# A two-layer hybrid trunk: the first loads in halves, ScalarE's rotary copies one level later, and the last scaling regrouped

## The chip, the cores and the metric

The kernel runs on one core of one Trainium2 chip. The metric is the device time of one execution in microseconds: the median of three runs was 838.24 us, from 836.58 to 839.73. All data is float32.

## What is computed

The reference is two layers and a last normalisation, on 256 tokens of 1024 features. Cut to what matters:

```python
def hybrid_layer(x, ...):
    h = rms_norm(x, norm_mix)
    proj = einsum('btd,dp->btp', h, w_in)       # 4120 columns
    y_gdn = gdn_mixer(...)      # 6 heads: conv, silu, l2norm, gated delta rule by chunks
    y_ret = retention_mixer(...)  # 4 heads: q and k are turned by rotary(), then retention
    y_mlstm = mlstm_mixer(...)  # 6 heads
    x = x + concat(y_gdn, y_ret, y_mlstm) @ w_out
    x = x + hierarchical_moe(rms_norm(x, norm_ffn), ...)   # 32 experts, top 2
    return x
# after both layers: rms_norm(x, norm_final)
```

`rotary(x)` returns `[x1*cos - x2*sin, x1*sin + x2*cos]` for the two halves x1, x2 of a head's 64 features. The gated delta rule needs the inverse of a unit lower triangular matrix for each head and half of the sequence.

## The kernel before, in words

The program is written engine by engine, with an explicit order in each engine's own queue and semaphores between them. An engine does what stands in its queue in that order; if one instruction waits, all behind it wait.

**Weights.** SyncE's queue (SP) issues nearly all loads. A slot holds 1 MB of weights (2048 float32 in each of 128 partitions). There are 12 ring slots and 12 more that are made from buffers free at the time. Each layer loads 24 slots of mixer weights (L484; `PROJ` gives their order: gdn 0, the small gates slot, gdn 1 to 4, gate 0 to 4, rqk 0 and 1, mv 0 and 1, mqk and so on) and 96 slots of expert weights (L511, three for each of 32 experts). A load waits until its slot was freed: `mix_freed` is counted up by TensorE, `moe_freed` by GpSimd. Among the loads SP also swaps the halves of the heads for the rotary step (`swap_halves`, L463 to L470: four small DMAs for the queries, before load 23 of the mixer, and four for the keys, before the third expert load); it waits there for ScalarE's copy (`rraw_ready`).

**The start.** SP loads the input as two halves of 512 KB (L461), then weight slot after weight slot, with the constants (1125 KB) after the third. ScalarE's queue loads `pars` (154 KB), the level masks (224 KB) and the router's weights (160 KB) at L1137 to L1139. ScalarE squares the two halves of x (L1146) while VectorE multiplies them with the gain into `hU` (L1434) and then sums the squares (L1443, L1444). TensorE's first product (gdn 0, L621) works on `hU`, which isn't normalised yet: the whole tile 0 (features k = 0 to 7), then k = 0 to 3 of tile 1, then the product with ones that gives the sum of squares (L629), then k = 4 to 7 of tile 1. ScalarE makes 1/rms from it (L1152, L1154), VectorE makes `hT` (L1448), and the products of all further slots (L597) read `hT`. A float32 matmul shows as two records of 256 columns in the profile, so 8 matmuls are "x16".

**The levels.** The inverse is built by doubling, in six levels (lev 1 to 6). In each, TensorE makes W (L800), transposes X (L780), runs half of a filler, makes Z (L813) and runs the other half of the filler. The filler is a product that the layer needs anyway: rqk 0 in levels 1 and 2, rqk 1 in levels 3 and 4, mv 0 in level 5, mv 1 in level 6. ScalarE copies the even columns of XT to XE before each level's transposes (L1234, two groups), waiting for VectorE's subtractions (L1625), and copies X out of PSUM behind the transposes (L1237). Behind L1237 ScalarE has one extra piece of work in each level:

```python
if lev == 2:
    rotary_in(0)                  # L1243: waits for rqk 0 in full, copies it (L1216)
if lev == 3:
    act.activation(mixT[:, 0:5, :], ..., ACT.Silu)
if lev == 4:
    rotary_in(1)                  # L1247
    act.preload_act_table_set(LN_EXP)
if lev > 4:
    values(("mv", lev - 5), ...)  # waits for the mv product of this level
```

VectorE turns the copies with cos and sin (`rotate`, L1587 to L1597) in level 4 for the queries and in level 6 for the keys, between its reads of W and its subtractions of Z; it waits there for the swapped halves (`partner_in`).

**The experts.** Both layers run eight groups of four experts, and one of them a second time for the tokens that did not fit, so 9 rounds in a layer. A round reads 12 slots, but the second turn of a group loads nothing.

**The end.** The last round leaves the result in PSUM banks 0 to 3 (bank 2j + h: token half j, feature half h). ScalarE squares them (L1377, L1380), makes 1/rms for j = 1 and then j = 0 (L1383, L1385). VectorE scales by 1/rms and gain in four operations (L1838), and SP issues one output DMA behind each (L516).

Of the kernel before, what the change touches and what calls it, by code (L numbers as in the profile page):

```python
# [30 lines left out]
P = 128  # L31
LAYERS = 2
D = 1024
# [12 lines left out]
RING = 12  # L46
SLOT = 2048
# [125 lines left out]
def trunk(nc, x_in, consts, level_masks, params, w_mix, router_w, e_gate, e_up, e_down, gain_final, row_store, out):  # L173
# [6 lines left out]
    with ExitStack() as ctx:  # L180
# [217 lines left out]
        const_in = sem("const_in")  # L398
        x_loaded = [sem(f"x_loaded{j}") for j in range(2)]
# [26 lines left out]
        out_ready = sem("out_ready")  # L426
        out_done = sem("out_done")
# [31 lines left out]
        def _(sync):  # L459
            for j in range(2):  # L460
                sync.dma_start(xT[:, 4 * j:4 * j + 4, :], x_in[:, 4 * j:4 * j + 4, :]).then_inc(x_loaded[j], 16)  # L461

# [9 lines left out]
            for l in range(LAYERS):  # L472
                for i in range(NMIX):
# [40 lines left out]
            for i, (j, h) in enumerate(((1, 0), (1, 1), (0, 0), (0, 1))):  # L514
# [39 lines left out]
        def _(pe):  # L554
# [52 lines left out]
            for l in range(LAYERS):  # L607
# [6 lines left out]
                have_slot(0)  # L614

                def first_tile(ct, ks):

                    for k in ks:
                        if ct == 0 and k % 2 == 0:
                            pe.wait_ge(hU_ready, upto(l, hU_ready, k // 2 + 1))  # L620
                        mm = pe.matmul(bank[:, ct * T:(ct + 1) * T], slot_w(0)[:, k, ct * P:(ct + 1) * P], hU[:, k, :],  # L621
                                       start=(k == 0), stop=(k == KD - 1))
                    return mm

                first_tile(0, range(KD))
                first_tile(1, range(4))
                sq_bank = begin("ssq")
# [472 lines left out]
        def _(act):  # L1100
# [37 lines left out]
            act.dma_start(lvl_raw, level_masks).then_inc(lvl_in, 16)  # L1138
            act.dma_start(rws[:, :, :], router_w[:, 0]).then_inc(rw_in, 16)  # L1139
            act.wait_ge(init_done, 2)  # L1140
            act.preload_act_table_set(LN_EXP)
            for l in range(LAYERS):
                if l == 0:
                    for i in range(2):
                        act.wait_ge(x_loaded[i], 16)
                        act.activation(sq_in[:, 4 * i:4 * i + 4, :], xT[:, 4 * i:4 * i + 4, :], ACT.Square).then_inc(squared, 2)  # L1146
                else:
# [79 lines left out]
                for lev in range(1, 7):  # L1227
# [14 lines left out]
                    if lev == 2:  # L1242
                        rotary_in(0)  # L1243
                    if lev == 3:
                        act.activation(mixT[:, 0:5, :], mixT[:, 0:5, :], ACT.Silu).then_inc(gate_ready, 1)
                    if lev == 4:
# [131 lines left out]
            for i, j in enumerate((1, 0)):  # L1378
# [6 lines left out]
                act.activation(ss[:, 4 + j:5 + j], ss[:, j:j + 1], ACT.Exp, scale=-0.5).then_inc(final_rstd, 1)  # L1385

        @block.vector
        def _(dve):
# [442 lines left out]
            dve.wait_ge(gfin_in, 16)  # L1831
            dve.wait_ge(final_sq, 2)
            dve.tensor_scalar(ss[:, 2:4], ss[:, 0:2], 1.0 / D, EPS, ALU.mult, ALU.add).then_inc(final_half, 1)
            for i, j in enumerate((1, 0)):
                dve.wait_ge(final_rstd, i + 1)
                for h in range(2):
                    part = slice(h * 512, (h + 1) * 512)
                    dve.scalar_tensor_tensor(out=fin[:, j, part], in0=ps[:, 2 * j + h, :], scalar=ss[:, 4 + j:5 + j],  # L1838
                                             in1=gfin[:, part], op0=ALU.mult, op1=ALU.mult).then_inc(out_ready, 1)
# [82 lines left out]
```

## Time and profile before

| what | us |
|---|---|
| median of three runs | 838.24 |
| the profiled execution | 839.36 |
| its span in the profile | 837.6 |
| PE busy (share of the span) | 783.1 (94%) |
| DVE busy | 307.2 (37%) |
| ACT busy | 201.3 (24%) |

PE is TensorE, DVE VectorE, ACT ScalarE, SP SyncE; PEq, SPq and so on are an engine's own queue. The durations below all come from the profiled execution, whose time stands 1.76 us over its span and 1.12 us over the median. The chain of waits follows the last instruction back to what released it, so its pieces add up to the span; the timeline lists what each engine did, with the idle time before it and what ended that in brackets; the waits sum idle time over an engine's instructions.

### The profile page before, as it was taken

To read this page: it belongs to the slowest core of one execution; us is meant where nothing else is said; L and a number is where in the kernel's file an instruction comes from. 1 tells how busy PE (TensorE), PEld (TensorE's weight loads), DVE (VectorE), ACT (ScalarE), POOL (GpSimd) and SP (SyncE) were. 2 spreads that over 40 slices of the span, in tenths; PEclk is the share of its full clock that TensorE was granted. 3 is DMA by queue.
4 is the path that set the end of the run, shared out by engine and by line. 5 is a ranking of instruction groups with operands and counts; after the bars stand their busy time and mean duration, and the time that the engine had idled before them with its cause. 6 is when DMAs were issued, how large, how long until landed. Compare 5 with 4: busy or idle time off the path is not lost.

```text
span 837.6 us, 16668 instructions
## 1 busy us (share of the span) xinstructions
PE 783.1 (94%) x6584; PEld 556.1 (66%) x6584; DVE 307.2 (37%) x733; ACT 201.3 (24%) x427; POOL 4.3 (1%) x13
## 2 busy tenths in 40 slices
PE   4999989999999998799999999899999999999966
PEld 4877778888765554455588778788787555454423
DVE  2757433564421111111177653436624111111102
ACT  2252551442300010001114445326212000001002
POOL 1000000000000000000000000000000000000000
PEclk9999999999999999699999999999999999999998
DMA  9851354486789999999996322645947999999995
GB/s 355 360 176 69 118 188 166 144 325 241 304 360 420 421 420 421 419 423 419 418 418 227 124 103 64 241 156 167 367 191 303 421 420 419 422 421 419 421 421 232
DMA packets 41065, 253.86 MB, mean 303 GB/s; under 512 B 4768, under 2 KB 9376, under 8 KB 11936
## 3 DMA queue, kind: packets, MB, share of 16 engines
q1 hardware_dynamic: 40416, 252.14, 75.4%
q8 instruction: 50, 0.82, 0.4%
q10 hardware_dynamic: 576, 0.72, 0.3%
q14 instruction: 23, 0.19, 0.1%
HBM read 250.35 MB, written 1.44 MB: 301 GB/s over the span
## 4 chain that ended last, share of the span: by engine, by line
PE 70%; DMA 11%; DVE 11%; ACT 3%; issue 3%; DVEq 1%; SPq 0%; ACTq 0%; POOLq 0%
PE ps L1049 13%; PE ps L597 12%; DMA ring<-e_up 10%; PE ps L1019 8%; PE ps L1070 7%; PE ps L921 6%; PE ps L768 4%; PE ps L1078 4%; PE ps L1082 3%; PE ps L813 2%; PE ps L621 2%; DVE xn L1421 2%; DVE work L1540 2%; PE ps L846 1%; PE ps L780 1%
## 5 line engine op out<-in xcount | busy, mean ns | idle before, releaser
L597 PE MATMUL ps<-hT,ring 128*128 128x256 f32 x800 | 183.4, 382 | 0.0
L597 PEld LDWEIGHTS ps<-hT,ring 128*128 128x128 f32 x800 | 148.3, 190 | 22.8 <-issue 3.8
L1019 PEld LDWEIGHTS ps<-work,xn 128*128 128x128 f32 x640 | 77.2, 201 | 10.3 <-issue 8.2
L1019 PE MATMUL ps<-work,xn 128*128 128x128 f32 x640 | 81.0, 288 | 1.9 <-DVE work L1759 1.9
L1049 PE MATMUL ps<-ring,hT 128*32 128x256 f32 x1088 | 67.0, 391 | 7.4 <-DMA ring<-e_up 7.4
L1049 PE MATMUL ps<-work,hT 128*32 128x256 f32 x960 | 59.9, 393 | 8.1 <-DMA work<-e_gate 5.7
L921 PE MATMUL ps<-xn,ring 128*128 128x256 f32 x256 | 57.8, 381 | 0.0
L1049 PEld LDWEIGHTS ps<-ring,hT 128*32 128x32 f32 x1088 | 34.5, 112 | 33.6 <-DMA ring<-e_up 10.5
L921 PEld LDWEIGHTS ps<-xn,ring 128*128 128x128 f32 x256 | 48.1, 190 | 7.2 <-issue 0.7
L1049 PEld LDWEIGHTS ps<-work,hT 128*32 128x32 f32 x960 | 28.9, 112 | 36.2 <-issue 12.1
L1759 DVE TENSOR_TENSOR work<-shapes,sel 128x128 f32<-128x128 f32 x40 | 9.9, 288 | 114.7 <-PE ps L1056 114.4
L1776 DVE TENSOR_TENSOR hT<-ps,pars 128x512 f32<-128x512 f32 x40 | 27.7, 692 | 52.9 <-PE ps L1019 52.9
L1364 ACT ACTIVATE work<-ps 128x256 f32<-128x256 f32 x18 | 6.9, 385 | 159.2 <-PE ps L1049 159.2
L1828 DVE COPY hT<-ps 128x512 f32<-128x512 f32 x18 | 12.4, 691 | 88.6 <-PE ps L1070 88.6
L1070 PE MATMUL ps<-ring,work 128*32 128x512 f32 x288 | 34.6, 598 | 8.5 <-ACT work L1368 8.5
L1368 ACT ACTIVATE work<-ps 128x256 f32<-128x256 f32 x18 | 6.9, 384 | 146.9 <-PE ps L1063 146.9
L768 PE MATMUL ps<-ring,hT 128*128 128x128 f32 (+1 forms) x256 | 37.5, 303 | 1.1 <-DVEq L1407 1.1
L1078 PEld LDWEIGHTS ps<-work,hT 128*128 128x128 f32 x144 | 25.1, 189 | 18.8 <-issue 7.5
L768 PEld LDWEIGHTS ps<-ring,hT 128*128 128x128 f32 x256 | 34.4, 191 | 3.9 <-DVEq L1407 1.9
L1078 PE MATMUL ps<-work,hT 128*128 128x256 f32 x144 | 36.1, 393 | 0.0
L1082 PE MATMUL ps<-hT,work 128*128 128x512 f32 x72 | 35.9, 621 | 0.0
L1625 DVE TENSOR_TENSOR work<-work,ps 128x192 f32<-128x192 f32 (+1 forms) x48 | 16.9, 353 | 33.7 <-PE ps L813 27.3
(283 smaller groups left out, 843.8 us busy)
## 6 DMA issues: line engine op xcount, KB each, us to landing
ring<-e_up SPq DMA_DIRECT2D x48, 1024.0 KB, 26.2
ring<-w_mix SPq DMA_DIRECT2D x34, 1024.0 KB, 9.6
ring<-e_down SPq DMA_DIRECT2D x32, 1024.0 KB, 26.0
work<-e_gate SPq DMA_DIRECT2D x32, 1024.0 KB, 20.2
more_buf<-e_gate SPq DMA_DIRECT2D x16, 1024.0 KB, 18.6
ring<-e_gate SPq DMA_DIRECT2D x16, 1024.0 KB, 18.7
work<-e_up SPq DMA_DIRECT2D x16, 1024.0 KB, 24.2
shapes<-e_down SPq DMA_DIRECT2D x8, 1024.0 KB, 21.9
```

What stands on the lines that cost most here:

```text
L597: mm = pe.matmul(bank, slot_w(i)[:, k, ct * P:(ct + 1) * P], hT3[:, k, :], start=(k == 0), stop=(k == KD - 1))
L621: mm = pe.matmul(bank[:, ct * T:(ct + 1) * T], slot_w(0)[:, k, ct * P:(ct + 1) * P], hU[:, k, :], start=(k == 0), stop=(k == KD - 1))
L768: mm = pe.matmul(bank[:, j * n:(j + 1) * n], hT3[:, k, j * P:(j + 1) * P], w[:, k, 0:n], start=(k == 0), stop=(k == KD - 1))
L813: mm = pe.matmul(z[j][0:rows_, i * HD:(i + 1) * HD], XC[half(j), h, 0:rows_], WC[half(j), h, :], start=True, stop=True)
L921: mm = pe.matmul(ps[:, b, i * T:(i + 1) * T], w[:, k, i * P:(i + 1) * P], mixT[:, k, :], start=(k == 0 and i == 0), stop=(k == KD - 1 and ...
L1019: mm = pe.matmul(ps[:, 4 + 3 * half_, kk * P:(kk + 1) * P], xn3[:, j, k * P:(k + 1) * P], Psel[:, j, :], start=(j == 0), stop=(j == TT - 1))
L1049: mm = pe.matmul(ps[32 * e:32 * e + 32, 5 + m, 0:DE], hq[:, k, 32 * e:32 * e + 32], w[:, c0:c0 + DE], start=(k == 0), stop=(k == KD - 1), ...
L1070: mm = pe.matmul(ps[32 * e:32 * e + 32, 5 + h, :], hmT[:, f, 32 * e:32 * e + 32], w[:, e * 512:(e + 1) * 512], start=(f == 0), stop=(f == ...
L1078: mm = pe.matmul(ps[:, k // 2, k % 2 * T:(k % 2 + 1) * T], ysb[:, h, k % 4 * P:(k % 4 + 1) * P], PwT[:, 0:T], start=False, stop=False, ski ...
L1082: mm = pe.matmul(ps[:, 2 * j + h, :], PwT[:, j * P:(j + 1) * P], ysb[:, h, :], start=False, stop=False, skip_group_check=True)
L1625: link(TTn(own, own, z, ALU.subtract))
L1776: TTn(hq[:, half * 4:half * 4 + 4, :], ps[:, 4 + 3 * half, :].rearrange("p (k s) -> p k s", k=4), gq[:, half * 4:half * 4 + 4].unsqueeze(2 ...
```

## The change

At the start the input and the first weight slot come in interleaved halves: x first half, weights first half, x second half, weights second half. TensorE first runs 10 products of the tile of ones with itself into bank 3, whose result is never read, then k = 0 to 3 of both tiles of gdn 0 from the first halves, and then k = 4 to 7 of tile 0; the rest follows as before. In layer 1 there is no split load and there are no such products, but the new order of k holds. The loads of the level masks and the router's weights move behind ScalarE's two squares.

In the levels the copy of the rotary queries moves from level 2 to level 3, ahead of the Silu, and the copy of the rotary keys from level 4 to level 5, together with the load of the activation table.

At the end VectorE multiplies the first feature halves (h = 0) with the gain before 1/rms is there, and scales the second halves with both as before. The first half of j = 1 is then scaled by 1/rms on VectorE, that of j = 0 on ScalarE, which also issues its output DMA; SP issues three.

```diff
             for j in range(2):
                 sync.dma_start(xT[:, 4 * j:4 * j + 4, :], x_in[:, 4 * j:4 * j + 4, :]).then_inc(x_loaded[j], 16)
-
+                part = slice(j * SLOT // 2, (j + 1) * SLOT // 2)
+                sync.dma_start(slot[first][:, part], w_mix[0, 0, :, part]).then_inc(arrived[first] if j else first_half, 16)
...
-                for i in range(NMIX):
+                for i in range(1 - l, NMIX):
...
-            for i, (j, h) in enumerate(((1, 0), (1, 1), (0, 0), (0, 1))):
+            for i, (j, h) in enumerate(((1, 1), (1, 0), (0, 1))):
...
-                have_slot(0)
+                if l == 0:
+                    for _ in range(WARM):
+                        pe.matmul(ps[:, 3, 0:P], ones[:, :], ones[:, :], start=True, stop=True)
+                    pe.wait_ge(first_half, 16)
+                else:
+                    have_slot(0)
...
-                first_tile(0, range(KD))
+                first_tile(0, range(4))
                 first_tile(1, range(4))
+                have_slot(0)
+                first_tile(0, range(4, KD))
...
             act.dma_start(pars[:, :, :], params).then_inc(par_in, 16)
-            act.dma_start(lvl_raw, level_masks).then_inc(lvl_in, 16)
-            act.dma_start(rws[:, :, :], router_w[:, 0]).then_inc(rw_in, 16)
...
                         act.activation(sq_in[:, 4 * i:4 * i + 4, :], xT[:, 4 * i:4 * i + 4, :], ACT.Square).then_inc(squared, 2)
+                    act.dma_start(lvl_raw, level_masks).then_inc(lvl_in, 16)
+                    act.dma_start(rws[:, :, :], router_w[:, 0]).then_inc(rw_in, 16)
...
-                    if lev == 2:
+                    if lev == 3:
                         rotary_in(0)
-                    if lev == 3:
                         act.activation(mixT[:, 0:5, :], mixT[:, 0:5, :], ACT.Silu).then_inc(gate_ready, 1)
-                    if lev == 4:
+                    if lev == 5:
                         rotary_in(1)
                         act.preload_act_table_set(LN_EXP)
...
+            act.wait_ge(final_rstd, 2)
+            act.wait_ge(gained_half, 2)
+            act.activation(fin[:, 0, 0:512], fin[:, 0, 0:512], ACT.Copy, scale=ss[:, 4:5]).then_inc(out_first, 1)
+            act.wait_ge(out_first, 1)
+            act.dma_start(out[:, 0, 0:512], fin[:, 0, 0:512]).then_inc(out_done, 16)
...
-            for i, j in enumerate((1, 0)):
-                dve.wait_ge(final_rstd, i + 1)
-                for h in range(2):
-                    part = slice(h * 512, (h + 1) * 512)
-                    dve.scalar_tensor_tensor(out=fin[:, j, part], in0=ps[:, 2 * j + h, :], scalar=ss[:, 4 + j:5 + j],
-                                             in1=gfin[:, part], op0=ALU.mult, op1=ALU.mult).then_inc(out_ready, 1)
+            dve.wait_ge(gfin_in, 16)
+            for j in (1, 0):
+                TTn(fin[:, j, 0:512], ps[:, 2 * j, :], gfin[:, 0:512], ALU.mult).then_inc(gained_half, 1)
+
+            def last_half(j):
+                dve.scalar_tensor_tensor(out=fin[:, j, 512:D], in0=ps[:, 2 * j + 1, :], scalar=ss[:, 4 + j:5 + j],
+                                         in1=gfin[:, 512:D], op0=ALU.mult, op1=ALU.mult).then_inc(out_ready, 1)
+
+            dve.wait_ge(final_rstd, 1)
+            last_half(1)
+            dve.wait_ge(gained_half, 1)
+            dve.tensor_scalar(fin[:, 1, 0:512], fin[:, 1, 0:512], ss[:, 5:6], None, ALU.mult).then_inc(out_ready, 1)
+            dve.wait_ge(final_rstd, 2)
+            last_half(0)
```

In the new code the wait for `gfin_in` stands behind the operation that halves the sums (`final_half`); before it stood ahead of it. The start flag of gdn 0 is set on its first product alone.

## Rows read from the trace of the kernel before

**Rows 1.** page of the profile: its head, and the DMA rate in 40 slices

```profile
span 837.6 us, 16668 instructions
...
GB/s 355 360 176 69 118 188 166 144 325 241 304 360 420 421 420 421 419 423 419 418 418 227 124 103 64 241 156 167 367 191 303 421 420 419 422 421 419 421 421 232
...
```

**Rows 2.** chain of waits, 0 to 60 us: start us, length us, what

```profile
...
1.65 8.79 DMA ring<-w_mix
...
10.53 7.54 PE ps L621 x24
18.07 0.43 PE ps L629 x2
18.50 1.73 PE ps L621 x8
...
```

**Rows 3.** timeline, 0 to 45 us: start us, length us, engine, line, names

```profile
...
0.87 0.10 POOL L523 MEMSET epsc<- 128x1 f32 x1
...
5.89 1.22 DVE L1434 TENSOR_TENSOR work<-xT,pars 128x1024 f32<-128x1024 f32 x1 [5.89 <-DMA pars<-params]
...
10.85 0.42 DVE L1444 TENSOR_TENSOR xn<-xn 128x256 f32<-128x256 f32 x1
...
```

**Rows 4.** instructions of L621 from 12.8 to 13.5 us: durations ns

```profile
...
L621 PE MATMUL ps<-work,ring x3: 631/631/631, 12.4 to 13.2; 128*128 128x256 f32 x3
...
```

**Rows 5.** instructions of L621 from 16 to 16.8 us: durations ns

```profile
...
L621 PE MATMUL ps<-work,ring x5: 379/379/379, 15.8 to 16.6; 128*128 128x256 f32 x5
...
```

**Rows 6.** the two input DMAs of L461: us from issue to landing

```profile
...
DMA to landing us min/median/max: 4.9/5.5/6.2
```

**Rows 7.** chain of waits, 84 to 137 us: levels' fillers, one stall

```profile
...
99.39 1.73 PE ps L597 x8
...
106.95 1.73 PE ps L597 x8
...
113.75 1.73 PE ps L597 x8
...
118.92 0.61 ACT work L1216
...
119.69 1.28 ACT L1248
...
122.59 1.79 PE ps L768 x16
...
```

**Rows 8.** waits of PE over the span: us in total, times, longest us

```profile
...
PE ps L780 <- ACT late_buf L1234: 6.9, 8, 1.9
...
```

**Rows 9.** timeline, 84 to 136 us, of ScalarE, SyncE and VectorE around the copies

```profile
...
105.23 2.69 SPq L470 DMA_DIRECT2D work<-late_buf  x4
...
109.21 1.27 ACT L1245 ACTIVATE xn<-xn 128x1280 f32<-128x1280 f32 x1
...
110.57 0.52 ACT L1234 ACTIVATE late_buf<-work 128x384 f32<-128x384 f32 x1
...
113.84 0.69 DVE L1591 TENSOR_TENSOR work<-work,shapes 128x512 f32<-128x512 f32 x1 [0.24 <-DVE work L1608]
...
119.59 2.57 SPq L470 DMA_DIRECT2D work<-work  x4
...
129.59 0.69 DVE L1591 TENSOR_TENSOR work<-work,shapes 128x512 f32<-128x512 f32 x1 [0.24 <-DVE work L1605]
...
```

**Rows 10.** DMA issues by line over the span: count, KB, median us to landing

```profile
...
work<-late_buf SPq DMA_DIRECT2D x8, 64.0 KB, 2.0
work<-work SPq DMA_DIRECT2D x8, 64.0 KB, 7.1
...
```

**Rows 11.** chain of waits, 812 to 838 us

```profile
...
790.40 26.73 DMA ring<-e_up
...
```

**Rows 12.** timeline, 815 to 838 us, the last results

```profile
...
832.30 2.73 DVE L1838 SCALAR_TENSOR_TENSOR work<-ps,ss,more_buf 128x512 f32<-128x512 f32 x4 [1.20 <-ACT ss L1385]
...
833.21 0.20 ACT L1385 ACTIVATE ss<-ss 128x1 f32<-128x1 f32 x1
```

More of the change, by code:

```diff
@@ L46 @@
 RING = 12
+WARM = 10
 SLOT = 2048
@@ L398, in trunk @@
         const_in = sem("const_in")
+        first_half = sem("first_half")
         x_loaded = [sem(f"x_loaded{j}") for j in range(2)]
@@ L426, in trunk @@
         out_ready = sem("out_ready")
+        out_first = sem("out_first")
+        gained_half = sem("gained_half")
         out_done = sem("out_done")
@@ L459, in _ @@
         def _(sync):
+            first = loads[0][0][0]
             for j in range(2):
                 sync.dma_start(xT[:, 4 * j:4 * j + 4, :], x_in[:, 4 * j:4 * j + 4, :]).then_inc(x_loaded[j], 16)
+                part = slice(j * SLOT // 2, (j + 1) * SLOT // 2)
+                sync.dma_start(slot[first][:, part], w_mix[0, 0, :, part]).then_inc(arrived[first] if j else first_half, 16)
             def swap_halves(a):
@@ L621, in first_tile @@
                         mm = pe.matmul(bank[:, ct * T:(ct + 1) * T], slot_w(0)[:, k, ct * P:(ct + 1) * P], hU[:, k, :],
-                                       start=(k == 0), stop=(k == KD - 1))
+                                       start=(k == 0 and ct == 0), stop=(k == KD - 1 and ct == 1), skip_group_check=True)
                     return mm
-                first_tile(0, range(KD))
+                first_tile(0, range(4))
                 first_tile(1, range(4))
+                have_slot(0)
+                first_tile(0, range(4, KD))
                 sq_bank = begin("ssq")
@@ L1829, in _ @@
                         dve.reg_add(rounds, rounds, 1)
-            dve.wait_ge(gfin_in, 16)
             dve.wait_ge(final_sq, 2)
             dve.tensor_scalar(ss[:, 2:4], ss[:, 0:2], 1.0 / D, EPS, ALU.mult, ALU.add).then_inc(final_half, 1)
-            for i, j in enumerate((1, 0)):
-                dve.wait_ge(final_rstd, i + 1)
-                for h in range(2):
-                    part = slice(h * 512, (h + 1) * 512)
-                    dve.scalar_tensor_tensor(out=fin[:, j, part], in0=ps[:, 2 * j + h, :], scalar=ss[:, 4 + j:5 + j],
-                                             in1=gfin[:, part], op0=ALU.mult, op1=ALU.mult).then_inc(out_ready, 1)
+            dve.wait_ge(gfin_in, 16)
[10 more added lines that the diff above has]
+            last_half(0)
 def kernel(**inputs):
```

## The prediction

> **What bounds the kernel now.** I read the page first. Its DMA line shows about 420 GB/s in most slices of the expert stages and much less in the mixers [rows 1], so what bounds has to be read stage by stage. The chain of waits comes next. In its first 60 us it is one DMA, weight slot 0, up to 10.4 us, and from 10.53 us TensorE's products with no gap [rows 2]. The chain of the levels is TensorE as well, but with a stretch of ScalarE inside: the copy of the rotary keys at 118.92 and a table load at 119.69, before TensorE's filler begins at 122.59 [rows 7]. Near the end of layer 1 the expert loads bound: the chain's step of 26.73 us is one of them, issued at 790.40 [rows 11]. The last 5 us are ScalarE's statistics and VectorE's four scalings [rows 12].
>
> Does time won early last? The saturated stretches begin when TensorE frees slots: before each of them the rate is lower (241 to 360 GB/s in slices 10 to 12, 191 and 303 in slices 30 and 31) [rows 1]. Their start moves with TensorE, and their length is given by bytes. So I take a shift of TensorE before them in full, in both layers. If I am wrong there, it is rival 3.
>
> **Part 1, the start.** Before, slot 0 was in at 10.44. The second x half was in at 1.19 + 6.2 = 7.4 and the first at 0.74 + 4.9 = 5.6 [rows 6]. VectorE's first hU took 1.22 us and was released by pars [rows 3]. Now the first x half and the first half of the weights stand where both x halves stood, 1 MB, and 384 KB of ScalarE's loads (masks, router) no longer run beside them. So the half weights are in by 7.4 at the latest. With x half 0 at 5.5 to 5.9 and 1.22 us for hU, TensorE can start between 6.7 and 7.4; I take 7.2.
>
> Prices of TensorE: 8 records take 1.73 us at the full rate [rows 2]. The first records lasted 631 ns against 379 ns later [rows 4, 5]: these are the two levels of the clock, 1.2 and 2.4 GHz, after an idle start. The first 24 records took 7.54 us against 3 x 1.73 = 5.19, so the slow start cost 2.35 us. The ten products of ones are 20 records of 128 columns, half of those above: 20 x 0.216 / 2 = 2.2 us at the full clock, 4.3 us at half. They can begin when GpSimd's two fills are done at 0.97 [rows 3], end near 5.4, and nothing waits for them; their cover is the wait for the first loads, and without it they would cost their 4.3 us. I take it that they bring the clock up and that it stays up over the idle 1.8 us to 7.2. No row shows such a gap at such a moment; the bounds are 0 and 2.35 us of loss.
>
> Then: 16 records from 7.2 to 10.7 (k = 0 to 3 of both tiles). The second x half now comes after 1.5 MB of SP's queue: slot 0 landed at 10.44 behind 2 MB, its last 512 KB take 1.25 us at 420 GB/s [rows 1] and the 384 KB of ScalarE's are gone (0.9), so 8.2; the whole of slot 0 near 9.5. The 8 records of tile 0, k = 4 to 7, run from 10.7 to 12.4 without a wait (hU for them: 8.2 + 1.22 = 9.4). The sum of squares was ready at 10.85 + 0.42 = 11.27 [rows 3], 3.9 us behind the second x half; so now at 12.1. The product with ones takes 0.43, the last 8 records 1.73: slot 1's work starts at 14.6, where it started at 18.50 + 1.73 = 20.23 [rows 2]. Gain 5.6 us. The sum of squares, near 12.1, caps it at 6.0; with the clock down it is 3.3. Slot gdn 1 is 2 MB + 128 KB + 1 MB into SP's queue, by 420 GB/s and slot 0's old landing about 12.9, ahead of 14.6. The constants (another 1125 KB) are wanted after two tiles and the gates, past 22. Masks and router weights, now issued near 9, are wanted tens of us later. In layer 1 the order of k changes nothing: the same 12 products stand ahead of the sum.
>
> A rule speaks against halving. By the Trainium skill, page "DMA: Bandwidth & Descriptors", section "Anatomy of one DMA — SWDGE (gpsimd) path", each DMA has a fixed part of about 2.0 us beside its bytes; if four DMAs paid it one after another, TensorE would start some 2 us later. The rows are against that here: the two x halves were issued 0.45 us apart and landed 1.8 us apart [rows 6], which 512 KB and ScalarE's share nearly fill by themselves.
>
> **Part 2, the rotary copies.** Level marks are the fillers' starts: 99.39, 106.95, 113.75, 122.59 [rows 7]. A level with no copy in its way is 113.75 - 106.95 = 6.80 us (level 3's filler to level 4's). Level 2 to 3 is 7.56, level 4 to 5 is 8.84. The excess is 0.76 and 2.04: the copy waits for the whole filler, then takes 0.61 (and the table load 1.28) ahead of the XE copies that the next transposes want. TensorE waited for XE copies 6.9 us in 8 places over the two layers [rows 8], so I take layer 1's levels to be like layer 0's. Moved one level on, a copy's source is long there and it runs in ScalarE's gap behind L1237. Gain 2.80 a layer, 5.6 us.
>
> What hides the moved work: in level 3 the Silu began at 109.21 and the XE copy at 110.57 [rows 9]; 0.65 us more ahead of it puts XE at 111.2, done 111.8, while the transposes come 0.8 us before the filler at 113.75, thus at 112.9. In level 5 copy and table load need 2.1 us before the mv copy, which waits 4 us for its product anyway.
>
> What comes late next is the swap of halves. SP issued the four queries' DMAs from 105.23 over 2.69 us, and each lands 2.0 after its issue [rows 9, 10]: 4.4 behind the copy. The copy now ends near 108.6 on the old marks, the swap at 113.0, and VectorE's rotate began at 113.84: 0.9 to spare. For the keys, copy end 122.2, four issues of 2.57 in all, landing near 126.5 to 127, also because three 1 MB loads stand ahead (7.1 from issue to landing before); rotate would begin at 129.59 - 2.04 = 127.6. Also hidden, by 0.6 or more. I cost both at nothing; without cover 0 to 1 us a layer, because VectorE would hold up its subtractions of Z. SP itself waits 3 us longer for the keys' copy with the expert loads 3 to 96 behind it. The third was not issued before 125.9, and the rate there was 144 to 188 GB/s (slices 6 to 8) [rows 1], so these loads catch up.
>
> **Part 3, the end.** VectorE's last operation ended at 832.30 + 2.73 = 835.03, with 0.68 each; the first 1/rms was there at 832.27, the second at 833.41 [rows 12]. Now two gain products (2 x 0.69) fill 831.1 to 832.5, then follow 0.68, the scaling in SBUF (no row; between 0.35 and 0.69, I take 0.5), and 0.68 with gaps of 0.05: 834.4. ScalarE scales its half from 833.4 to 834.1 and issues it meanwhile. The last DMA goes out 0.6 us earlier (0.3 to 0.8).
>
> **Sum.** 5.6 + 5.6 + 0.6 = 11.8 us, against the profiled execution 839.36 - 11.8 = 827.6. That one stood 1.12 over the median, so 826.4 for the median.
>
> **Rivals.**
> 1. The early products do not bring the clock up, or it falls again in the gap. For: the gap of 1.8 us, and the products' 4.3 us are hardly longer than the 4 us of slow records before [rows 2, 4]. Against: no row shows a fall after so short a gap. Price 2.35: 828.8. The Trainium skill ("TensorE: Matmul & The Clock Gate", "The HAM clock gate (the "warmup" mystery)") says that the slow start is a matter of time, not of the number of matmuls, and varies from run to run; by that, this rival would hold in some executions.
> 2. The swapped halves come late, and VectorE waits in levels 4 and 6. For: margins of 0.9 and 0.6 us. Price up to 1 us a layer: about 828.
> 3. The expert loads end the kernel on their own clock and take back what TensorE wins in front: the saturated stretches start no earlier. Then only part 3 and some of layer 0's stall remain, 837 or so. Against: the low rates ahead of them [rows 1].
> 4. Slower: SP stands at the wait for the keys' copy while slots are free, so expert loads are missing when a saturated stretch begins. Each 1 MB costs 2.5 us at 420 GB/s; five or more in all must be late to eat 11.8 us, and at seven the time is 843. It decides from the point where SP is held for 12 us or more beyond the free slots. I find 3 us against low rates.
>
> **How the numbers follow.** All three parts as worked: 0.55, time 826.4, alone 825 to 828. Rival 1: 0.2. Rival 2: 0.15. Rival 3: 0.07. Rival 4: 0.02. The last 0.01 is for a change that does nothing. The range takes in the first three with both together (831) and the bounds of the prices: 824.6 to 831.5. About 0.5% (4.2 us) is what a measurement of this kernel can tell from no change: faster 0.93, same 0.05, slower 0.02.
>
> **What would show it.** Right: the first L621 record near 7.2 at 379 ns, L597 starting near 14.6, all levels' marks 6.8 to 7 apart up to level 5, no ScalarE copy in the levels' chain, the fillers of layer 1 some 8.4 us earlier before its own levels, and saturated stretches of unchanged length. Wrong: L621 records of 631 ns after 7.2 (rival 1); an idle VectorE before L1591 with the swap as releaser (rival 2); the expert rounds' starts shifted but the end not (rival 3); lower DMA rates where they were 420 (rival 4).

## The result, and the profile after

| | before | after |
|---|---|---|
| median, us | 837.81 (4 runs, 836.58 to 839.73) | 827.47 (4 runs, 825.73 to 828.91) |
| profiled execution, us | 839.36 | 828.05 |
| its span, us | 837.6 | 826.2 |

The ratio is 0.9876, with a 95% interval from 0.9855 to 0.9897: between 8.6 and 12.1 us were won, where 11.8 us were forecast. Line numbers below are those of the changed kernel: L621 became L632, L597 became L603.

**The start.** The chain of waits of the changed kernel from 0 to 60 us (start, length, what) answers to [rows 2]:

```profile
...
6.93 7.02 PE ps L632 x24
13.94 0.43 PE ps L642 x2
14.37 1.73 PE ps L632 x8
16.10 3.71 PE ps L603 x16
...
```

TensorE's first real product starts at 6.93 instead of 10.53, but slot 1's work only at 16.10 instead of 20.23. That is 4.1 us, not 5.6. The timeline of the same stretch has the products of ones, and the two groups below it are the records of L632 from 9 to 10 and from 11 to 12 us, as [rows 4] and [rows 5]:

```profile
...
1.02 4.63 PE L622 MATMUL ps<-ones 128*128 128x128 f32 x20 [1.02 <-POOL epsc L529]
...
11.33 0.42 DVE L1462 TENSOR_TENSOR xn<-xn 128x256 f32<-128x256 f32 x1
...
```

```profile
...
L632 PE MATMUL ps<-work,ring x3: 634/634/634, 8.8 to 9.6; 128*128 128x256 f32 x3
...
```

```profile
...
L632 PE MATMUL ps<-work,ring x6: 379/379/379, 10.8 to 11.8; 128*128 128x256 f32 x6
...
```

Records of 634 ns still start at 9.6 us, 8.6 us after the products of ones began. The first 24 records took 7.02 us, where 5.19 is the price at the full clock: 1.8 us were lost in this execution, where it was 2.35 before. The lower clock is read from the records here. The profile's granted clock stands at 1.00 over the first 20 us of every kernel, also where the records are long.

**The levels.** The chain from 80 to 132 us, the levels' fillers as in [rows 7]:

```profile
...
95.27 1.73 PE ps L603 x8
...
102.06 1.73 PE ps L603 x8
...
108.85 1.73 PE ps L603 x8
...
115.64 1.79 PE ps L781 x16
...
123.11 1.79 PE ps L781 x16
...
127.72 3.46 PE ps L603 x16
...
```

The marks are 6.79, 6.79, 6.79 and 7.47 us apart; the levels 2 to 3 and 4 to 5 have lost their 0.77 and 2.05 us, and up to 115.64 no ScalarE stands in between. The last step, level 5 to 6, was 7.46 before too: the chain has ScalarE's copy of the mv product there, in both kernels. One thing came as not forecast. VectorE in level 6 (timeline, 76 to 132 us):

```profile
...
124.44 0.69 DVE L1609 TENSOR_TENSOR work<-work,shapes 128x512 f32<-128x512 f32 x1 [2.04 <-DMA work<-work]
...
```

It waits 2.04 us for the swapped keys, 1.4 us in layer 1. But the chain goes on from 127.72 at its old pace.

**The experts.** Some starts that can be laid over each other, us from the span's start:

| start of | before | after | earlier by |
|---|---|---|---|
| slot 1's first product | 20.22 | 16.09 | 4.1 |
| first product behind the levels, layer 0 (u1) | 137.96 | 131.01 | 6.95 |
| first expert product, layer 0 | 230.94 | 224.01 | 6.9 |
| layer 1's first product | 421.54 | 414.70 | 6.8 |
| u1, layer 1 | 546.85 | 537.20 | 9.65 |
| gather ahead of layer 1's experts | 636.08 | 626.43 | 9.65 |
| first expert product, layer 1 | 641.46 | 630.20 | 11.3 |
| last 16 records of L1049 (now L1062) | 817.18 | 805.90 | 11.3 |
| end of the last product | 831.85 | 820.47 | 11.4 |
| end of the span | 837.6 | 826.2 | 11.4 |

In this pair the shift of layer 0's start and levels goes through both layers unchanged, through both stalls on expert loads. But the table has a step that is no part of the change: 1.6 us between the gather and the first expert product of layer 1. The chain over the span, before and then after:

```profile
...
636.08 5.45 PE ps L1019 x32
641.53 3.59 PE ps L1049 x64
...
```

```profile
...
626.43 3.84 PE ps L1032 x32
630.27 3.59 PE ps L1062 x64
...
```

The same 32 records took 5.45 us before and 3.84 after: the execution profiled before ran them partly at the lower clock (granted 0.52 from 636 to 638 us and 0.63 from 638 to 640). It is a matter of the execution, as the experiments show. So the change as such was worth 9.8 us in this pair of profiles.

**The end.** The timeline of the last us, answering to [rows 12], and the landing of SP's three output DMAs and of ScalarE's:

```profile
...
820.92 0.75 DVE L1856 SCALAR_TENSOR_TENSOR work<-ps,ss,more_buf 128x512 f32<-128x512 f32 x1
...
822.06 0.72 ACT L1401 ACTIVATE work<-work,ss 128x512 f32<-128x512 f32 x1
822.06 0.75 DVE L1856 SCALAR_TENSOR_TENSOR work<-ps,ss,more_buf 128x512 f32<-128x512 f32 x1
822.81 0.38 ACTq L1403 DMA_DIRECT2D out<-work  x1
```

```profile
...
DMA to landing us min/median/max: 2.1/2.4/3.0
```

```profile
...
DMA to landing us min/median/max: 2.8/2.8/2.8
```

VectorE ends at 822.81, which is 2.34 us after TensorE's last product instead of 3.18. But the span's end is 5.73 us after that product, as against 5.75. The DMA rate in slices of 0.125 us, before from 833 us and after from 821.62 us, which is the same distance from the end of the last product (1.15 us):

```profile
...
GB/s 0 0 0 0 0 0 0 164 426 377 393 328 443 344 426 328 393 393 361 426 328 410 328 459 344 442 328 426 344 181 0 0 0 0 0 0 0 0 0 0
...
```

```profile
...
GB/s 0 0 0 0 0 0 0 164 442 344 393 377 426 328 360 393 360 426 361 426 344 410 377 393 360 426 328 394 361 197 0 0 0 0 0 0 0 0 0 0
...
```

The megabyte flows from the eighth slice to the thirtieth in both. With the four DMAs closer together each one only takes longer to land, up to 3.0 us instead of 2.1.

### The profile page after: what moved, and what is told of

Same layout as the page of the kernel before. It is cut to its first block, busy times and chain, and to the rows that moved or that the text cites. A ratio compares the mean times of both kernels' runs of the same rounds, so it can differ in the third digit from the quotient of the medians.

```text
span 826.2 us, 16713 instructions
## 1 busy us (share of the span) xinstructions
PE 784.9 (95%) x6604; PEld 557.0 (67%) x6604; DVE 307.7 (37%) x734; ACT 201.9 (24%) x428; POOL 3.1 (0%) x13
## 3 DMA queue, kind: packets, MB, share of 16 engines
HBM read 250.35 MB, written 1.44 MB: 305 GB/s over the span
## 4 chain that ended last, share of the span: by engine, by line
PE 68%; DMA 15%; DVE 11%; issue 3%; ACT 3%; DVEq 0%; SPq 0%; ACTq 0%; POOLq 0%
DMA ring<-e_up 14%; PE ps L603 12%; PE ps L1062 11%; PE ps L1032 7%; PE ps L1083 6%; PE ps L934 6%; PE ps L781 4%; PE ps L1091 3%; PE ps L1095 3%; PE ps L826 2%; PE ps L632 2%; DVE xn L1439 2%; DVE work L1558 2%; PE ps L859 1%; PE ps L793 1%
## 5 line engine op out<-in xcount | busy, mean ns | idle before, releaser
L603 PE MATMUL ps<-hT,ring 128*128 128x256 f32 x800 | 183.4, 382 | 0.0
L603 PEld LDWEIGHTS ps<-hT,ring 128*128 128x128 f32 x800 | 148.3, 190 | 22.9 <-issue 3.8
L1032 PEld LDWEIGHTS ps<-work,xn 128*128 128x128 f32 x640 | 74.4, 195 | 10.3 <-issue 8.2
L1032 PE MATMUL ps<-work,xn 128*128 128x128 f32 x640 | 78.2, 281 | 1.9 <-DVE work L1777 1.9
L1062 PE MATMUL ps<-ring,hT 128*32 128x256 f32 x1088 | 67.2, 391 | 4.9 <-DMA ring<-e_up 4.8
L1062 PE MATMUL ps<-work,hT 128*32 128x256 f32 x960 | 60.7, 397 | 10.4 <-DMA work<-e_gate 5.7
L1062 PEld LDWEIGHTS ps<-ring,hT 128*32 128x32 f32 x1088 | 34.4, 112 | 32.0 <-DMA ring<-e_up 9.0
L1062 PEld LDWEIGHTS ps<-work,hT 128*32 128x32 f32 x960 | 29.1, 113 | 38.9 <-issue 12.6
L1843 DVE TENSOR_TENSOR work<-work,ps 128x256 f32<-128x256 f32 x18 | 7.6, 421 | 57.7 <-PE ps L1062 57.7
```

Of the source, the lines that this page charges most:

```text
L603: mm = pe.matmul(bank, slot_w(i)[:, k, ct * P:(ct + 1) * P], hT3[:, k, :], start=(k == 0), stop=(k == KD - 1))
L1032: mm = pe.matmul(ps[:, 4 + 3 * half_, kk * P:(kk + 1) * P], xn3[:, j, k * P:(k + 1) * P], Psel[:, j, :], start=(j == 0), stop=(j == TT - 1))
L1062: mm = pe.matmul(ps[32 * e:32 * e + 32, 5 + m, 0:DE], hq[:, k, 32 * e:32 * e + 32], w[:, c0:c0 + DE], start=(k == 0), stop=(k == KD - 1), ...
```

## The experiments

Each kernel of this study also has GpSimd clamp its loaded count of extra rounds at zero:

```diff
+            nclamp = pool.alloc_register("pool_clamp")
...
-                    pool.reg_add(rounds, rounds, nreg)
+                    pool.reg_alu(nclamp, nreg, 0, ALU.max)
+                    pool.reg_add(rounds, rounds, nclamp)
```

The ratio of times is always to the kernel before on the same chip, with its 95% interval.

**The start alone.** The hunks of the change for SP's first loads, TensorE's first tile and ScalarE's loads, put into the kernel before.

> The kernel before with the change at the start alone. GpSimd clamps its loaded count at zero in every kernel of this study, which is one register operation in eight places of a layer and off TensorE's path. Theory A (a shift of TensorE ahead of the saturated loads is kept to the end): slot 1's work starts near 16.1 us instead of 20.2, and the time is 3.5 to 4.5 us under that of before. Rival B (the expert loads end the kernel on their own clock): the same start, but less than 1 us in the time. In both, the records of the first product last 631 ns for some 3 us after 6.9 us.

Measured: 833.35 us against 837.56, ratio 0.9959 (0.9941 to 0.9977), 3.4 us (1.9 to 4.9). Its timeline from 0 to 14 us:

```profile
...
6.87 5.42 PE L632 MATMUL ps<-work,ring 128*128 128x256 f32 x24 [1.21 <-DVE work L1447]
...
```

Here the 24 records took 5.42 us, close to the full clock, and slot 1's work started at 14.45. The expectation, taken from the one profile after, missed that; the prediction's 14.6 was right for this execution. Its u1 came 117.84 us behind slot 1's start (before 117.74), and from the first expert product of layer 1 to the last product of the up weights it took 175.7 us, like before: behind slot 1's start this profile kept the shift. The time is another matter. Slot 1's work started 5.8 us earlier than in the profile before, but the time fell by 3.4 us, and the interval ends at 4.9. The profiled execution was the fastest of the ten (831.31 us, the others 832.43 to 835.97), so it need not stand for them. The granted clock over the whole span, known for each execution, was 0.980 to 0.982 in the four slowest (835.30 us and more) and 0.984 to 0.989 in the six others: clock losses behind the start, which differ from execution to execution, are in these times too.

**The rotary copies alone.** The hunks in ScalarE's levels, put into the kernel before.

> The kernel before with the two rotary copies one level later, alone. Theory A: each layer's levels are 2.8 us shorter, 5.6 us in the time; VectorE waits 1 to 2 us for the swapped keys in level 6 of each layer, and it costs TensorE nothing because the first product behind the levels covers it. Rival B (late loads take it back): 2.8 us or less in the time. Rival C (VectorE's wait is on the path): 3.5 us or less, with TensorE idle behind level 6.

Measured: 832.35 against 837.56 us, ratio 0.9936 (0.9913 to 0.9960), 5.4 us (3.4 to 7.3). From slot 1's start to u1: 21.14 to 136.06, 114.92 us against 117.74, so 2.8 us; in layer 1 from the first product to u1 122.54 against 125.31. VectorE's wait was there, 1.9 and 1.7 us:

```profile
...
129.34 0.69 DVE L1592 TENSOR_TENSOR work<-work,shapes 128x512 f32<-128x512 f32 x1 [1.89 <-DMA work<-work]
...
```

Theory A holds, and VectorE's wait costs nothing at this size.

**The end alone.**

> The kernel before with the change at the end alone. Theory D: the four output DMAs of 256 KB are bound by their bytes, 1 MB in about 2.6 us from the first issue, and the first issue comes as long after TensorE's last product as before; so from that product's end to the end of the span there are 6.6 us as before, within 0.1, although VectorE ends 0.8 us earlier. Rival E (the last issue sets the end): the span ends 0.6 us nearer to the last product. The time itself is within its noise in both.

Measured: 838.72 against 837.56 us, ratio 0.9997 (0.9979 to 1.0015). From the end of TensorE's last product to the end of the span 5.77 us (the expectation's 6.6 counted from another record; by this one, before has 5.75). As theory D has it: VectorE is done earlier, and the span isn't.

**The whole change again.**

> The whole change, with GpSimd's clamp only added, as the base for the further runs: 9.5 to 11.5 us under before. If the three parts add up, it equals their sum within 1 us. If the gain has a part that none of the three holds, such as a stretch of TensorE at the lower clock at the head of layer 1's experts (before, the gather there took 5.45 us against 3.84 in the changed kernel), then that stretch differs from run to run in both kernels.

Measured: 826.27 against 837.56 us, ratio 0.9856 (0.9824 to 0.9888), 12.1 us (9.4 to 14.7), a little more than expected. The 24 records took 5.42 us, slot 1's work started at 14.61, u1 at 129.52. The gather ahead of the experts took 3.84 us in both layers, so the slow one of the profile before is no part of the change. The three parts alone give 0.41 + 0.64 + 0.03 = 1.08%, the whole 1.44%, and their intervals overlap. The clamp shows no cost.

**No products of ones, and 14.** `WARM = 0` and `WARM = 14` in the whole change.

> The whole change with no products of ones. Theory F (the ten products shorten the slow stretch little, because the clock is still low when the first real product starts, and rises about 3 us later): the 631 ns records last about 4 us from 6.9 us as before the change, and slot 1's work starts 0 to 0.7 us later than with ten. Rival G (the products are what makes the first product fast): 2 us or more later.

> The whole change with 14 products of ones, so that they last to about 7.5 us at the lower clock and TensorE has no gap before the first real product. Theory F (the gap of 1.3 us put the rise off): the rise comes before or soon after 7.5 us, the 24 records take 5.2 to 6 us instead of 7.0, and slot 1's work starts 0.5 to 1.5 us earlier than with ten. Rival H (products of ones, all equal, do not count for the clock): the first real product starts 0.5 us later, its slow stretch stays about 3 to 4 us, and slot 1's work starts 0.3 to 1 us later than with ten.

Measured: 828.81 us with none (ratio 0.9886, 0.9858 to 0.9914), 826.90 with 14 (0.9870, 0.9840 to 0.9899). The intervals overlap, but the profiles differ. The first products of the two kernels:

```profile
...
7.12 7.84 PE L634 MATMUL ps<-work,ring 128*128 128x256 f32 x24 [7.12 <-DVE work L1454]
...
```

```profile
...
1.03 5.12 PE L624 MATMUL ps<-ones 128*128 128x128 f32 x28 [1.03 <-POOL epsc L529]
6.97 5.42 PE L634 MATMUL ps<-work,ring 128*128 128x256 f32 x24 [0.82 <-DVE work L1454]
...
```

The 14 products ended at 6.15 us, not near 7.5 as expected: their 28 records took 5.12 us, while 20 took 4.63. Their first ones last 421 ns and their last ones 275 ns, so the clock had risen before they ended, and a gap of 0.82 us was left. The same is seen at the end of the ten in the kernel with the swap first, below (20 records in 4.34 us). In the other profiles with ten products all 20 records are slow, also where the first real product is fast; there the clock rose in between.

Over all profiled executions of this study the 24 records took:

| products of ones | gap ahead of the first real product, us | 24 records, us |
|---|---|---|
| none (before, rotary alone, end alone, queries alone, table alone, `WARM = 0`) | no work before | 7.54, 8.36, 8.29, 7.14, 6.89, 7.84 |
| 10 (after, the start alone, the whole again, swap first, keys in level 6) | 1.2 to 1.7 | 7.02, 5.42, 5.42, 5.42, 5.42 |
| 14 (`WARM = 14`, the last kernel) | 0.8 and 1.0 | 5.42, 5.45 |
| 10, slot 0 in one piece | 3.8 | 7.47 |

So theory F fell: without the products slot 1's work started at 17.11 against 14.61 with them, 2.5 us, as rival G said. Against the profile after, with 16.10, it is 1.0; that one was the odd one out among five. In the times, whose intervals overlap, the 2.5 us are not shown. That 14 do better than 10 is not shown: both gave 5.42, and one miss in five against none in two is no difference.

**Slot 0 in one piece.**

```diff
             for j in range(2):
                 sync.dma_start(xT[:, 4 * j:4 * j + 4, :], x_in[:, 4 * j:4 * j + 4, :]).then_inc(x_loaded[j], 16)
-                part = slice(j * SLOT // 2, (j + 1) * SLOT // 2)
-                sync.dma_start(slot[first][:, part], w_mix[0, 0, :, part]).then_inc(arrived[first] if j else first_half, 16)
+            sync.dma_start(slot[first], w_mix[0, 0]).then_inc(arrived[first], 16)
...
-                    pe.wait_ge(first_half, 16)
+                    have_slot(0)
```

> The whole change, but slot 0 loaded in one piece behind both halves of x. TensorE's first real product then waits for it: it starts near 9.6 us, 0.9 us earlier than before the change because ScalarE's two loads are out of the way, and slot 1's work starts 1.5 to 2.5 us later than with halves. If the halves were worth nothing, because the sum of squares (ready near 11.8 us) or the clock sets the start of slot 1's work, it would start within 0.5 us of the halves' 16.1.

Measured: 829.78 us (ratio 0.9898, 0.9869 to 0.9928).

```profile
...
9.43 7.47 PE L634 MATMUL ps<-work,ring 128*128 128x256 f32 x24 [3.77 <-DMA ring<-w_mix]
...
```

The first real product starts at 9.43 and slot 1's work at 19.06, which is 4.4 us later than with halves at the full clock, more than the 1.5 to 2.5 expected. The halves are worth their 2.4 us of earlier start. The other 2 us are the low clock behind the gap of 3.8 us. That the gap is its cause isn't shown: this is one execution, and the profile after had a slow first product behind 1.3 us. The median lies 2.7 to 2.9 us above those of the swap first and of the 14 products, on the same chip, and not 4.4.

**The swap first.** `if m == 2:` ahead of `swap_halves(1)` becomes `if m == 0:`.

> The whole change, with the swap of the rotary keys issued ahead of the first two expert loads instead of behind them. Theory I: VectorE's wait for the swapped keys in level 6 (2.0 and 1.4 us with the change) is caused by 2 or 3 MB of weights ahead of them in the queue; it shrinks to under 0.5 us, the two expert loads come some 6 us later, and the time is the same within 0.2%, since the product behind the levels covered the wait. Rival J (the wait was on the path): TensorE leaves the levels 0.5 to 1 us earlier in each layer.

Measured: 827.13 us (ratio 0.9875, 0.9848 to 0.9903). From slot 1's start to u1 114.91 us, as in the whole change. The timeline from 112 to 130 us:

```profile
...
115.91 2.51 SPq L476 DMA_DIRECT2D work<-work  x4
...
118.46 1.09 SPq L517 DMA_DIRECT2D more_buf<-e_gate  x2
...
121.18 0.69 DVE L1611 TENSOR_TENSOR work<-work,shapes 128x512 f32<-128x512 f32 x1 [0.24 <-DVE work L1625]
...
```

VectorE's wait for the DMA is gone (the swapped keys land 2.0 us after their issue), and the time is the same. Theory I holds.

**The queries' copy alone, and the table load alone**, in the kernel before:

```diff
-                    if lev == 2:
+                    if lev == 3:
                         rotary_in(0)
-                    if lev == 3:
```

```diff
                     if lev == 4:
                         rotary_in(1)
+                    if lev == 5:
                         act.preload_act_table_set(LN_EXP)
```

> The kernel before with the copy of the rotary queries alone moved from level 2 to level 3. Theory A: level 2 to 3 falls from 7.56 to 6.8 us, level 4 to 5 stays at 8.84; each layer's levels are 0.76 us shorter, 1.5 us in the time, at the edge of what three rounds tell. Rival: the copy delays the Silu in level 3 and with it level 4, and the gain moves there: levels as long as before.

> The kernel before with the table load alone moved from level 4 to level 5, both copies left where they were. Theory A: level 4 to 5 falls by the table load's 1.28 us, from 8.84 to 7.56, no more, since the copy of the keys still stands there; 2.6 us in the time over both layers. Rival: the table load hardly counts and the copy's wait for the filler does; the level falls by less than 0.5 us.

Measured: 839.06 against 839.05 us (ratio 1.0003, 0.9984 to 1.0021) and 835.50 (0.9958, 0.9941 to 0.9975), so nothing for the queries' copy and 3.5 us (2.1 to 4.9) for the table load, where 1.5 and 2.6 were expected. The fillers' starts in the chain of layer 0, queries' copy alone and then table load alone:

```profile
...
99.20 1.73 PE ps L599 x8
...
105.99 1.73 PE ps L599 x8
...
112.78 1.73 PE ps L599 x8
...
121.63 1.79 PE ps L770 x16
...
```

```profile
...
98.88 1.73 PE ps L599 x8
...
106.46 1.73 PE ps L599 x8
...
113.25 1.73 PE ps L599 x8
...
120.84 1.79 PE ps L770 x16
...
```

Levels 2 to 3 and 4 to 5 are 6.79 and 8.85 in the first, 7.58 and 7.59 in the second. In layer 0 the levels do what theory A says: 0.77 us for the first copy, 1.25 for the table load, and so 0.80 for the second copy. The queries' 1.5 us over two layers don't appear in the time, and its interval, which ends at 1.3 us, leaves them out. The profile shows what took them back in its execution. From layer 1's first product to u1 it took 126.47 us, where 125.31 less 0.77 would be 124.5. The transposes behind ScalarE's copy and table load, before and then with the queries' copy alone, and the granted clock (the last but two) behind them in the second:

```profile
...
530.55 0.93 PE L780 MATMUL ps<-shapes,late_buf 128*128 128x128 f32 x6 [1.92 <-ACT late_buf L1234]
...
```

```profile
...
529.66 1.51 PE L782 MATMUL ps<-shapes,late_buf 128*128 128x128 f32 x6 [1.92 <-ACT late_buf L1236]
...
```

```profile
...
529.60:534.00 4.40, 4.34 (x24) 4.25 (x26) 0.00 (x0) 1.31 (x3) 0.00 (x0) 0.61 0.99 365
...
```

TensorE was idle for the same 1.92 us in both, and in the second its clock was low behind it, which cost 1.9 us. The other executions have no profile, but each has its granted clock over the whole span: 0.980 to 0.984 in nine of the ten, against 0.984 to 0.989 in the 18 of the kernel before on this chip. This points to the clock as what took the gain back; in which stretches of the others, and why more than before, isn't shown. The whole change has no such idle time in its levels, and so not this loss.

**The keys' copy in level 6**, in the whole change:

```diff
                     if lev == 5:
+                        act.preload_act_table_set(LN_EXP)
+                    if lev == 6:
                         rotary_in(1)
-                        act.preload_act_table_set(LN_EXP)
```

> The whole change with the copy of the rotary keys yet one level later, in level 6, to find where VectorE's wait for the swapped halves begins to cost. VectorE then waits some 6 us in level 6 instead of 1 to 2. Theory K (the slack is about 2 us of the Z product and 2 us of the first mqk product): TensorE now stands idle behind level 6 for 2 to 3 us in each layer, and the time is 4 to 6 us over the whole change. Rival (the wait is covered however long): the same time.

Measured: 836.69 against 839.05 us, ratio 0.9964 (0.9945 to 0.9983). That is some 9 us over the whole change (0.9856), more than was expected; the spans are 834.9 and 824.7 us. The chain from 124 to 150 us, and the windows around the stall (start:end, length, busy us of PE, PEld, DVE, ACT and POOL, then PEclk, DMA share and GB/s):

```profile
...
126.34 3.46 PE ps L605 x16
129.79 2.03 issue
131.83 2.54 PE ps L839 x12
134.36 5.83 PE ps L605 x16
...
```

```profile
...
120.00:129.60 9.60, 9.17 (x92) 8.20 (x86) 2.79 (x5) 2.90 (x6) 0.00 (x0) 1.00 0.36 114
129.60:131.80 2.20, 0.20 (x1) 0.00 (x1) 1.39 (x4) 0.00 (x0) 0.00 (x0) 1.00 0.98 398
131.80:134.00 2.20, 2.17 (x12) 2.20 (x12) 0.07 (x1) 0.00 (x0) 0.00 (x0) 0.57 0.48 194
134.00:140.00 6.00, 6.00 (x18) 4.91 (x18) 0.00 (x0) 0.49 (x1) 0.00 (x0) 0.59 0.48 175
140.00:150.00 10.00, 10.00 (x61) 8.80 (x62) 4.17 (x9) 1.44 (x4) 0.00 (x0) 1.00 0.30 103
...
```

VectorE waited 6.3 us; 4.3 us of it were covered and 2.03 us left TensorE idle. Behind that gap its clock was granted at 0.57 to 0.59, so that two steps which take 1.28 and 3.51 us in the whole change took 2.54 and 5.83. The stretch from u1 to layer 0's first gather was 92.6 us against 89.2. So the visible stall cost 2.3 us in layer 0 (u1 at 131.83 against 129.52), and the clock another 3.4. In layer 1 it was 2.2 and 1.8 us. Theory K's stall of 2 to 3 us came as expected; the time was missed because it left out the clock.

**A last kernel:** the whole change with 14 products of ones, `hU` in two pieces for each half, and the first output in two pieces:

```diff
-WARM = 10
+WARM = 14
...
-                        TTn(hU[:, ks, :], xT[:, ks, :], gained(ks), ALU.mult).then_inc(hU_ready, 2)
+                        for k in (4 * j, 4 * j + 2):
+                            ks = slice(k, k + 2)
+                            TTn(hU[:, ks, :], xT[:, ks, :], gained(ks), ALU.mult).then_inc(hU_ready, 1)
...
-            last_half(1)
+            last_half(1, 512, 768)
+            last_half(1, 768, D)
```

> The whole change with 14 products of ones, hU made in two pieces for each half of x, and the first output issued in two pieces of 128 KB, the first as soon as 256 columns are scaled. TensorE's first real product should start 0.5 us earlier, near 6.5 us, unless the first half of the weights isn't there yet. By theory D (the output is bound by its bytes from the first issue) the stretch from TensorE's last product to the end falls by 0.3 us from 5.75; if the last issue or the scalings set the end, it doesn't change. Together 0.3 to 0.8 us under the whole change, which the times alone can't show.

Measured: 826.58 against 839.05 us, ratio 0.9848 (0.9826 to 0.9870); it can't be told from the whole change. Its first real product:

```profile
...
7.04 5.45 PE L634 MATMUL ps<-work,ring 128*128 128x256 f32 x24 [0.96 <-DMA ring<-w_mix]
...
```

No kernel of the study beats the changed one by more than its interval. The first product starts at 7.04, now released by the first half of the weights, so `hU` was not the only bound. The stretch behind the last product was 5.86 us. Theory D, as it stood, missed here: the first issue came 0.98 instead of 1.23 us behind the last product, but the end did not come nearer. The DMA rate from 820 us, again in slices of 0.125 us, has a dip to 172 GB/s behind its start:

```profile
...
GB/s 0 0 0 0 0 0 0 0 131 336 336 222 172 352 344 189 262 377 328 426 344 426 328 459 311 442 344 426 360 377 393 328 328 49 0 0 0 0 0 0
...
```

It fits a queue that had run out of data to send: the output would then be bound by its bytes only as long as the scalings keep up.

## Why the prediction was right, point by point

**The shift is kept.** The prediction took a shift ahead of the saturated loads in full. It holds: from the first expert product of layer 1 to the last product of the up weights, before 175.7 us, after 175.7, and in the kernels with one part alone or the whole 175.6 to 175.9, in spite of starts up to 13 us apart. In layer 0, from its first expert product to layer 1's first product, all kernels lie between 189.2 and 191.0 us, in no order of their starts. Rivals 3 and 4 are out.

**Part 1, the start, 5.6 us.** The steps up to the first product were within 0.3 us: 6.93 for 7.2, and the sum of squares at 11.75 for 12.1. What failed in the profile after is the step "I take it that they bring the clock up and that it stays up over the idle 1.8 us". Rival 1 was true in that execution, for 1.8 of its 2.35 us, and slot 1's work started at 16.1 instead of 14.6. But in four of the five profiled executions with ten products the step held, and the start was 14.45 to 14.72. The idle time behind the products was 1.2 to 1.7 us, not 1.8. Rival 1 was to hold in some executions; it held in one of the five. The slow stretch without the products is also not the fixed 2.35 us that one profile showed: the six values of 6.89 to 8.36 us lie 1.7 to 3.2 us over 5.19. The gain is therefore a spread, from 4.1 us up in the profiles. In the times it is smaller: the start alone gave 3.4 us (1.9 to 4.9), which leaves out the 5.6. A lower clock behind the start in four of its ten executions has a share in that; the rest stays open. That a fixed cost of each DMA doesn't stop the halves also held: the first product started at 9.43 in one piece and at 6.9 to 7.15 in halves. The section of the Trainium skill that the prediction names for that cost is on DMAs issued by GpSimd; the loads here are issued by SyncE.

**Part 2, the rotary copies, 5.6 us.** 2.8 us in each layer in the profile, 5.4 in the time of this part alone. The step on the swap was wrong: "Also hidden, by 0.6 or more". VectorE waited 2.04 and 1.4 us, so rotate began 1.4 to 2 us later than it could. The prediction had the swapped keys land 4.3 to 4.8 us behind the end of their copy. They came 7.1 us behind it: the copy ended at 117.31, and rotate was released at 124.44. The loads ahead in the queue made the difference, since with the swap issued ahead of them each of its DMAs landed 2.0 us after its issue. The wait costs nothing because a second cover stood behind it, which the prediction did not name: TensorE has half of mv 1 and the 3.46 us of the first mqk product to do before it needs the last level. With the keys' copy in level 6 this cover was used up at some 4.3 us of wait. So rival 2 had its wait, and no price.

**Part 3, the end, 0.6 us.** Wrong: it gave 0.0 (5.73 against 5.75, and 5.77 alone). The step that failed is "The last DMA goes out 0.6 us earlier", taken as the end. VectorE did end 0.8 us nearer to the last product, and the DMAs were issued sooner, but four of 256 KB take 2.85 us from their first byte at the 370 GB/s measured, and the first issue did not move. The prediction had looked at issues and not at bytes. No run changed the number of bytes, so this cause is read from the rates and isn't tested by itself.

**The sum.** 11.8 us against 10.3 between the medians; parts 1 and 3 were too large by about 1.5 (in one execution) and 0.6. The median of 827.47 came 1.1 above the 826.4. The sum also started from one execution before that carried 1.6 us of slow gather in layer 1, which no part of the prediction had separated. So part of the nearness is luck: 11.4 us lie between the two spans, but the change has only 9.8 of them. Against the profile of the whole change again, with the clock up at the start, it is 12.9 less the same 1.6, so 11.3, where parts 1 and 2 together were forecast at 11.2.

## What to carry to other kernels

A wait of a side engine should be costed against the next thing that the main engine needs from it, over all the work that stands between; here 2 us of it were free and 6 us were not. When the main engine does go idle, add what the lower clock may cost behind the gap; here it was 3.4 and 1.8 us behind gaps of 2.0. And at the end of a kernel, count the bytes of the output from its first issue before shortening the arithmetic in front of the last one.

## What the runs showed of the hardware

- A gap of 2.03 us on TensorE, after busy work, was followed by a granted clock of 0.57 to 0.59 over some 8 us (L605: 16 records in 5.83 instead of 3.51 us), and its twin of 2.02 us in layer 1 by 0.68 to 0.78 over 6 us. The Trainium skill ("TensorE: Matmul & The Clock Gate", "HAM oscillation — how this bites in real kernels") tells of a kernel whose waits for DMAs throttle TensorE again and again. The trace agrees that a wait does it, but the waits of that kernel are longer; here 2.03 us were enough.
- The gap's length alone does not decide. The kernels with both the keys' copy and the table load in level 4 (before, the start alone, the end alone, queries alone) have a gap of 1.92 to 1.94 us in each layer, and one of these eight was followed by the lower clock (0.61 over 4.4 us). What else decides isn't shown.
- Behind the products of ones, with gaps of 0.8 to 1.7 us, the next 24 records ran at about the full clock in six of seven executions; behind a gap of 3.8 us, in the one that has it, they did not.
- Products of the tile of ones with itself, whose result nobody reads, raise the clock: the 24 records behind them took 5.42 to 5.45 us in six of seven executions with short gaps, and 6.89 to 8.36 without them.
- The gather ahead of the experts ran at a partly lower clock in 7 of 28 chances (14 profiled executions, two layers): 5.33 to 5.47 us instead of 3.84. Kernels with and without the change had it, in layer 0 or in layer 1. The router's products just ahead had it in 6 others of the 28 (the stretch from u1 to the gather 90.4 to 90.5 us instead of 89.2). What decides it stays open; a comparison of two single profiles is off by 1.6 or 1.2 us where only one has it.
